# The FFN down product of a hybrid encoder layer: its sums in the order S3, S2, S1 and T3, T2, T1, and its products in that order

## The chip, the cores and the metric

One core of a Trainium2 chip runs the whole layer as one program. The metric is the device time of that core in microseconds (us), taken as the median of three runs.

## What is computed

The reference is one inference step of a streaming encoder layer on 1024 prompt rows and 32 sample rows: a combined input projection, latent attention beside an RWKV-7 state update, an output projection with a residual, and a SwiGLU feed-forward part. Everything is float32. The change touches the last step alone:

```python
def layer_tail(x, attn, rw, attn_out_g, w_out, norm_ffn_g, w_gate, w_up, w_down):
    mix = jnp.concatenate([rmsnorm(attn, attn_out_g), rw], axis=-1)
    h = x + mix @ w_out
    u = rmsnorm(h, norm_ffn_g)
    return h + (jax.nn.silu(u @ w_gate) * (u @ w_up)) @ w_down
```

The model width is 1024, the hidden width 2816, and there are 1056 rows.

## The kernel before

The function `tail` computes this last step, transposed: `hid` holds the hidden activations as 22 blocks of 128 partitions by 1056 rows, and `io.w_down` holds the weights by blocks of 128 output columns. The down product is done by the seven-product form of Strassen's method (Winograd's order of the sums), one level deep. The weights are split into A11, A12 (output blocks 0 to 3, hidden blocks 0 to 10 and 11 to 21) and A21, A22 (output blocks 4 to 7), the activations into B11, B12, B21, B22 by hidden half and row half. The sums are

- S1 = A21 + A22, S2 = S1 - A11, S3 = A11 - A21, S4 = A12 - S2, made by GpSimd (POOL), once in each round;
- T1 = B12 - B11, T2 = B22 - T1, T3 = B22 - B12, T4 = B21 - T2, made by VectorE (DVE), once for each of two column halves.

There are eight rounds n (list `DOWN`: two column halves `nh` by four output block pairs `j`). A round multiplies 128x128 blocks with 264 columns. It has seven products of 11 blocks (22 matmul instructions, since each block is given in two passes), which accumulate in four PSUM banks X, Y, Z and W; rounds alternate between two sets of four banks. Their names are those of the semaphores which they raise. In a round from the second on their order is

| product | operands | bank | what it waits for |
|---|---|---|---|
| q1 | A11, B11 | X | load `a11_in` |
| q6 | S2, T2 | Y | sums `e2_ok`, `f2_ok` |
| q7 | S3, T3 | Z | sums `e3_ok`, `f3_ok` |
| q5 | S1, T1 | W | stands behind q6, so nothing more |
| q4 | A22, T4 | Z | load `a22_in`, sum `f4_ok`, DVE's `q_u3` |
| q2 | A12, B21 | X | load `a12_in` |
| q3 | S4, B22 | W | sum `e4_ok`, DVE's `q_c22` |

In round 0, q2 stands right behind q1. DVE adds the products: u2 = Y + (a copy of q1's X), u3 = Z + u2, c22 = W + u3, then the four output tiles `yout`, each scaled and added to the residual tile `hres`.

What sets the order around the change is written out by hand, engine by engine:

- SyncE (SP) issues all loads from one queue in program order: A11 into `Alo[:, 0:FH]` (L2268), in round 0 also A12 (L2270), A21 into `Ahi[:, 0:FH]` (L2274), A22 into `Ahi[:, FH:]` (L2278), A12 into `Alo[:, FH:]` (L2282), then the stores of the round before (L2291) and the residual loads (L2294). There is one buffer of each; a load waits for the product and the sums that last read it. `FH` is 11.
- In round 0 A11 and A12 are loaded ahead of the end of the gate and up product, A21 and A22 behind its last product (`w_ps`).
- POOL makes the sums of a round in the order S1 (L2505, L2506: it lies in two places, so two instructions), S2 (L2510, L2511), S3 in place over A21 (L2512), S4 (L2517). Before S1 it waits for all of A11, A21 and A22.
- DVE makes T1 (L2642), T2 (L2643), T3 in place over B12 (L2644), T4 (L2647, L2648), for the first column half in front of round 0 and for the second within round 3.

All matmuls stand in the trace under line L2337 of a helper, and products are told apart by their tiles: q6 and q5 in one stretch are `psum<-mixT,u_sum`, q4 is `psum<-u_sum,wA`, q3 `psum<-hid,mixT`, and q1, q2 and q7 `psum<-hid,wA`. Where two products on the same tiles follow each other, one row shows the start of the first.

Of the kernel before, what the change touches and what calls it, by code (L numbers as in the profile page):

```python
# [7 lines left out]
ALU = mybir.AluOpType  # L8
# [2161 lines left out]
def tail(nc, g, io, phase):  # L2170
# [7 lines left out]
    FH, KH = FB // 2, KD // 2  # L2178
# [36 lines left out]
    S2d = u_sum[2][:, 0:FH * P].rearrange("p (k n) -> p k n", k=FH)  # L2215
# [15 lines left out]
    @block.sync  # L2231
    def _(sp):
        def load(u, b):
            sp.dma_start(wo[b], io.w_out[u]).then_inc(s[f"in{b}"], 16)

        for i, (a, b) in enumerate(X_PARTS):
            sp.dma_start(hT[:, a:b], io.x_cols[a:b].rearrange("k p n -> p k n")).then_inc(s[f"x_in{i}"], 16)
            if i:
                load(i + 1, i + 1)
        sp.dma_start(g_ffn[:, :], io.g_ffn).then_inc(s["g_in"], 16)  # L2240

        def load_unit(u):
            pair, b = u // 2, u % 2
            w = io.w_up if b else io.w_gate
            for a in range(2):
                sp.dma_start(ab[b][:, a], w[pair + a * FH]).then_inc(s[f"w_in{b}"], 16)

        load_unit(0)
        load_unit(1)
        for u in range(4, KD):  # L2250
            sp.wait_ge(s["ps_done"], 3 * (u - 3))
            load(u, u % 4)
        sp.wait_ge(s["h_ok"], 3 * KD)
        sp.dma_start(io.y.rearrange("k p n -> p k n"), hT).then_inc(s["h_st"], 16)
        for u in range(2, UNITS):
            sp.wait_ge(s["w_ps"], 2 * u - 2)
            load_unit(u)

        def rows(j):
            return io.w_down[j]  # L2260

        for n, (nh, j) in enumerate(DOWN):
            sp.wait_ge(s["w_ps"], 2 * UNITS - 2)
            if n:
                sp.wait_ge(s["q1_ps"], n)
                sp.wait_ge(s["e3_ok"], n)
                sp.wait_ge(s["e2_ok"], n)
            sp.dma_start(Alo[:, 0:FH], rows(j)[:, 0:FH]).then_inc(s["a11_in"], 16)  # L2268
            if n == 0:
                sp.dma_start(Alo[:, FH:], rows(j)[:, FH:]).then_inc(s["a12_in"], 16)  # L2270
            sp.wait_ge(s["w_ps"], 2 * UNITS)
            if n:
                sp.wait_ge(s["q7_ps"], n)
            sp.dma_start(Ahi[:, 0:FH], rows(j + KH)[:, 0:FH]).then_inc(s["a21_in"], 16)  # L2274
            if n:
                sp.wait_ge(s["q4_ps"], n)
                sp.wait_ge(s["e1_ok"], n)
            sp.dma_start(Ahi[:, FH:], rows(j + KH)[:, FH:]).then_inc(s["a22_in"], 16)  # L2278
            if n:
                sp.wait_ge(s["q2_ps"], n)  # L2280
                sp.wait_ge(s["e4_ok"], n)
                sp.dma_start(Alo[:, FH:], rows(j)[:, FH:]).then_inc(s["a12_in"], 16)  # L2282
            if n == 0:
                sp.wait_ge(s["h_st"], 16)
            else:
                sp.wait_ge(s["y_ok"], 3 * n)
                sp.wait_ge(s["q_x"], n)
                pn, pj = DOWN[n - 1]
                for a in range(4):
                    m, t0 = pj + KH * (a // 2), HT * (a % 2) + NW * pn  # L2290
                    sp.dma_start(io.y[m][:, t0:t0 + NW], yout[:, a, :]).then_inc(s["y_st"], 16)  # L2291
            for a in range(4):
                m, t0 = j + KH * (a // 2), HT * (a % 2) + NW * nh
                sp.dma_start(hres[:, a, :], io.y[m][:, t0:t0 + NW]).then_inc(s["res_in"], 16)  # L2294
        sp.wait_ge(s["y_ok"], 3 * len(DOWN))
        sp.wait_ge(s["q_x"], len(DOWN))
        pn, pj = DOWN[-1]
        for a in range(4):
            m, t0 = pj + KH * (a // 2), HT * (a % 2) + NW * pn
            sp.dma_start(io.y[m][:, t0:t0 + NW], yout[:, a, :]).then_inc(s["y_st"], 16)  # L2300
        sp.wait_ge(s["y_st"], 64 * len(DOWN))
        sp.wait_ge(s["h_st"], 16)

    @block.tensor
    def _(pe):
# [90 lines left out]
        for n, (nh, j) in enumerate(DOWN):  # L2396
            X, Y, Z, W = (4 * (n % 2) + i for i in range(4))
            c0, c1 = slice(nh * NW, nh * NW + NW), slice(HT + nh * NW, HT + nh * NW + NW)
            lo0, lo1 = (lambda k: hid[:, k, c0]), (lambda k: hid[:, k, c1])
            hi0, hi1 = (lambda k: hid[:, FH + k, c0]), (lambda k: hid[:, FH + k, c1])  # L2400
            left = lambda w: (lambda k: w[:, k, :])
            pe.wait_ge(s["a11_in"], 16 * n + 16)
            if n == 0:
                pe.wait_ge(s["hid_ok"], 6 * UNITS)
            if n >= 2:
                pe.wait_ge(s["q_x"], n - 1)
            product(X, left(Alo[:, 0:FH]), lo0, FH, "q1_ps")

            def x_close():
                pe.wait_ge(s["a12_in"], 16 * n + 16)  # L2410
                pe.wait_ge(s["q1_ok"], n + 1)
                product(X, left(Alo[:, FH:]), hi0, FH, "q2_ps", first=False)

            if n == 0:
                x_close()
            pe.wait_ge(s["e2_ok"], n + 1)
            pe.wait_ge(s["f2_ok"], nh + 1)
            if n >= 2:
                pe.wait_ge(s["q_u2"], n - 1)
            product(Y, left(S2d), lambda k: T2d[:, k, :], FH, "q6_ps")  # L2420
            pe.wait_ge(s["e3_ok"], n + 1)
            pe.wait_ge(s["f3_ok"], nh + 1)
            if n >= 2:
                pe.wait_ge(s["q_z"], n - 1)
            product(Z, left(Ahi[:, 0:FH]), lo1, FH, "q7_ps")
            if n >= 2:
                pe.wait_ge(s["q_w"], n - 1)
            product(W, lambda k: S1d[0][:, k, :] if k < 10 else S1d[1][:, k - 10, :], lambda k: T1d[:, k, :], FH, "q5_ps")
            pe.wait_ge(s["f4_ok"], nh + 1)
            pe.wait_ge(s["a22_in"], 16 * n + 16)  # L2430
            pe.wait_ge(s["q_u3"], n + 1)
            product(Z, left(Ahi[:, FH:]), lambda k: T4d[0][:, k, :] if k < 8 else T4d[1][:, k - 8, :], FH, "q4_ps", first=False)
            if n:
                x_close()
            pe.wait_ge(s["e4_ok"], n + 1)
            pe.wait_ge(s["q_c22"], n + 1)
            product(W, left(S4d), hi1, FH, "q3_ps", first=False)
# [44 lines left out]
    def _(pool):  # L2482
# [16 lines left out]
        for n in range(len(DOWN)):  # L2499
            pool.wait_ge(s["a11_in"], 16 * n + 16)  # L2500
            pool.wait_ge(s["a21_in"], 16 * n + 16)
            pool.wait_ge(s["a22_in"], 16 * n + 16)
            if n:
                pool.wait_ge(s["q5_ps"], n)
            tt(S1d[0], Ahi[:, 0:10], Ahi[:, FH:FH + 10], ALU.add)  # L2505
            tt(S1d[1], Ahi[:, 10:FH], Ahi[:, FH + 10:], ALU.add).then_inc(s["e1_ok"], 1)  # L2506
            pool.wait_ge(s["e1_ok"], n + 1)
            if n:
                pool.wait_ge(s["q6_ps"], n)
            tt(S2d[:, 0:10], S1d[0], Alo[:, 0:10], ALU.subtract)  # L2510
            tt(S2d[:, 10:], S1d[1], Alo[:, 10:FH], ALU.subtract).then_inc(s["e2_ok"], 1)  # L2511
            tt(Ahi[:, 0:FH], Alo[:, 0:FH], Ahi[:, 0:FH], ALU.subtract).then_inc(s["e3_ok"], 1)  # L2512
            pool.wait_ge(s["a12_in"], 16 * n + 16)
            pool.wait_ge(s["e2_ok"], n + 1)
            if n:
                pool.wait_ge(s["q3_ps"], n)
            tt(S4d, Alo[:, FH:], S2d, ALU.subtract).then_inc(s["e4_ok"], 1)  # L2517

    @block.vector
    def _(dve):  # L2520
        tt, stt = dve.tensor_tensor, dve.scalar_tensor_tensor

        def named(ins, name, value):
            ins.then_inc(s[name], 1)
            dve.wait_ge(s[name], value)
# [108 lines left out]
        for n, (nh, j) in enumerate(DOWN):  # L2634
            c0, c1 = slice(nh * NW, nh * NW + NW), slice(HT + nh * NW, HT + nh * NW + NW)

            def sums(nh):
                c0, c1 = slice(nh * NW, nh * NW + NW), slice(HT + nh * NW, HT + nh * NW + NW)
                B11, B12, B21, B22 = (hid[:, FH * a:FH * a + FH, c] for a in range(2) for c in (c0, c1))
                if nh:  # L2640
                    dve.wait_ge(s["q5_ps"], KH)
                named(tt(T1d, B12, B11, ALU.subtract), "f1_ok", nh + 1)  # L2642
                named(tt(T2d, B22, T1d, ALU.subtract), "f2_ok", nh + 1)  # L2643
                tt(B12, B22, B12, ALU.subtract).then_inc(s["f3_ok"], 1)  # L2644
                if nh:
                    dve.wait_ge(s["q4_ps"], KH)
                tt(T4d[0], B21[:, 0:8], T2d[:, 0:8], ALU.subtract)  # L2647
                tt(T4d[1], B21[:, 8:], T2d[:, 8:], ALU.subtract).then_inc(s["f4_ok"], 1)  # L2648
# [157 lines left out]
```

## Time and profile before

| | us |
|---|---|
| median of the runs (3) | 1897.72 |
| lowest and highest | 1897.05, 1898.7 |
| the profiled execution | 1898.8 |
| its span, first to last instruction | 1897.0 |
| TensorE matmul busy in the span | 1795.9 |
| VectorE busy | 955.3 |
| GpSimd busy | 691.5 |

The down product fills the last 290 us of the span or so. Start times are in us from the span's start. PE is the matmul, PEld the load of its weights, which runs just ahead of the matmul and marks where a product begins; PEclk is the granted clock of TensorE as a share of full speed.

### The profile page before, as it was taken

To read this page: it belongs to the slowest core of one execution; us is meant where nothing else is said; L and a number is where in the kernel's file an instruction comes from. 1 tells how busy PE (TensorE), PEld (TensorE's weight loads), DVE (VectorE), ACT (ScalarE), POOL (GpSimd) and SP (SyncE) were. 2 spreads that over 40 slices of the span, in tenths; PEclk is the share of its full clock that TensorE was granted. 3 is DMA by queue.
4 is the path that set the end of the run, shared out by engine and by line. 5 is a ranking of instruction groups with operands and counts; after the bars stand their busy time and mean duration, and the time that the engine had idled before them with its cause. 6 is when DMAs were issued, how large, how long until landed. Compare 5 with 4: busy or idle time off the path is not lost. (4 is left out here: it accounts for less than half of the span.)

```text
span 1897.0 us, 34197 instructions
## 1 busy us (share of the span) xinstructions
PE 1795.9 (95%) x14597; PEld 1336.5 (70%) x14597; DVE 955.3 (50%) x1710; ACT 384.9 (20%) x918; POOL 691.5 (36%) x495
## 2 busy tenths in 40 slices
PE   5999999999997987999899899999999999899998
PEld 3566666666665664555566788888888888688887
DVE  2757767766776773555333543343444334324422
ACT  2333333334333322333100111100001000000000
POOL 2553664555354534445320111222222220534522
PEclk9999999999997888999999999999999999999999
DMA  9343244324221006110130211101111112233331
GB/s 377 111 152 103 77 136 135 94 88 157 92 80 54 7 7 163 46 45 1 75 128 9 105 45 45 35 32 45 45 45 45 45 45 73 84 114 115 122 101 64
DMA packets 70906, 158.62 MB, mean 84 GB/s; under 512 B 19290, under 2 KB 47786, under 8 KB 66531
## 3 DMA queue, kind: packets, MB, share of 16 engines
q1 hardware_dynamic: 66866, 115.74, 19.0%
q10 hardware_dynamic: 3888, 40.70, 6.0%
q8 instruction: 116, 1.90, 0.4%
q14 instruction: 36, 0.29, 0.0%
HBM read 128.30 MB, written 20.44 MB: 78 GB/s over the span
## 5 line engine op out<-in xcount | busy, mean ns | idle before, releaser
L2337 PE MATMUL psum<-mixT,wA 128*128 128x264 f32 x1408 | 337.3, 388 | 1.9 <-DVE rb L2579 1.5
L2337 PEld LDWEIGHTS psum<-mixT,wA 128*128 128x128 f32 x1408 | 268.3, 191 | 48.6 <-DVE rb L2579 1.7
L2337 PE MATMUL psum<-u_sum,wA 128*128 128x264 f32 x1232 | 297.4, 386 | 0.5 <-DVE u_sum L2562 0.5
L437 PE MATMUL psum<-wsl,xt 128*128 128x368 f32 (+1 forms) x1092 | 283.8, 452 | 8.8 <-DMA wsl<-in_w_in 5.7
L2337 PEld LDWEIGHTS psum<-u_sum,wA 128*128 128x128 f32 x1232 | 234.3, 190 | 41.1 <-issue 0.9
L437 PEld LDWEIGHTS psum<-wsl,xt 128*128 128x128 f32 (+1 forms) x1092 | 150.0, 172 | 90.8 <-issue 18.1
L2492 POOL TENSOR_TENSOR wA<-wA 128x512 f32<-128x512 f32 x22 | 28.6, 1299 | 427.6 <-DMA wA<-in_w_gate 233.4
L2337 PE MATMUL psum<-hid,wA 128*128 128x264 f32 x528 | 121.6, 386 | 2.1 <-DVE hid L2630 1.5
L2337 PEld LDWEIGHTS psum<-hid,wA 128*128 128x128 f32 x528 | 100.2, 190 | 19.9 <-issue 2.8
L2505 POOL TENSOR_TENSOR u_sum<-wA 128x1280 f32<-128x1280 f32 x8 | 24.7, 3092 | 184.6 <-DMA wA<-in_w_down 184.6
L2337 PE MATMUL psum<-mixT,u_sum 128*128 128x264 f32 x352 | 82.9, 392 | 9.4 <-POOL u_sum L2511 9.4
L2130 DVE TENSOR_REDUCE part<-psum 128x1 f32<-128x80 f32 (+6 forms) x112 | 49.8, 470 | 76.2 <-PE psum L1924 73.8
L1278 POOL TENSOR_TENSOR Ls<-Lraw,con 128x512 f32<-128x512 f32 x45 | 49.2, 1102 | 106.5 <-ACT Lraw L945 76.5
L2337 PEld LDWEIGHTS psum<-mixT,u_sum 128*128 128x128 f32 x352 | 67.8, 193 | 22.4 <-POOL u_sum L2511 10.6
L1924 PE MATMUL psum<-kT,qT 96*128 96x144 f32 (+6 forms) x224 | 67.9, 463 | 7.8 <-DMA kT<-scratch_kT 7.8
L1244 POOL TENSOR_TENSOR st<-st,con 128x3 f32<-128x3 f32 (+1 forms) x18 | 50.7, 2816 | 60.2 <-DVE st L1441 30.7
L1943 PE MATMUL psum<-qT,kT 128*128 128x512 f32 (+6 forms) x224 | 71.4, 474 | 0.0
L2459 ACT ACTIVATE p<-psum 128x264 f32<-128x264 f32 x44 | 17.2, 390 | 253.6 <-PE psum L2337 253.4
L945 ACT ACTIVATE proj<-psum,rstd 128x368 f32<-128x368 f32 (+1 forms) x72 | 36.9, 512 | 136.5 <-PE psum L437 132.5
L1924 PEld LDWEIGHTS psum<-kT,qT 96*128 96x128 f32 x224 | 42.4, 197 | 30.0 <-DMA kT<-scratch_kT 7.9
L2092 POOL TENSOR_TENSOR tot<-tot,pT 128x832 f32<-128x832 f32 (+5 forms) x48 | 61.8, 1287 | 3.8
L1943 PEld LDWEIGHTS psum<-qT,kT 128*128 128x128 f32 x224 | 39.7, 183 | 31.5 <-issue 20.1
(362 smaller groups left out, 2875.9 us busy)
## 6 DMA issues: line engine op xcount, KB each, us to landing
wsl<-in_w_in ACTq DMA_DIRECT2D x27, 1472.0 KB, 6.9
wA<-in_w_down SPq DMA_DIRECT2D x32, 704.0 KB, 4.1
wA<-in_w_gate SPq DMA_DIRECT2D x22, 512.0 KB, 4.4
wA<-in_w_up SPq DMA_DIRECT2D x22, 512.0 KB, 4.4
mixed<-proj SPq DMA_DIRECT2D x8, 784.0 KB
xt<-in_x_tiles SPq DMA_DIRECT2D x9, 512.0 KB, 6.0
wsl<-in_w_in SPq DMA_DIRECT2D x3, 1472.0 KB, 11.3
out_y<-hid SPq DMA_DIRECT2D x1, 4224.0 KB, 12.0
```

The costliest lines, as they stand in the source:

```text
L437: return pe.matmul(out, lhsT, rhs, start=start, stop=stop)
L945: copy = lambda out, in_, **k: act.activation(out, in_, ACT.Copy, **k)
L1244: tt(out, ms, c_("minus_half")[:, 0:n], ALU.pow).then_inc(s[ok], 1)
L1278: tt(Ls[i % 2][:, :, :], Lraw[:, :, :], bcast(c_("levels")[:, i * 64:(i + 1) * 64], 1, H), ALU.mult).then_inc(s["Ls_ok"], 1)
L1924: pe.matmul(bank(pos)[:, 0:y - x], qT[b][0:QKD, t * P:(t + 1) * P], kT[b][0:QKD, x:y], start=True, stop=True).then_inc(s["a_ps"], 1)
L1943: pe.matmul(bank(pos)[0:size[k], 0:y - x], kT[b][:, k * P:k * P + size[k]], qT[b][:, x:y], start=True, stop=True).then_inc(s["b_ps"], 1)
L2092: step(pool.tensor_tensor(out[:, first[k]:], out[:, first[k]:], p[:, at[k]:at[k + 1]], ALU.add))
L2130: last = dve.tensor_reduce(part[:, t, slot:slot + 1], src[:, 0:w], AX.X, ALU.max)
L2337: ins = pe.matmul(pb[bank][:, 0:NW], left(k), right(k), start=first and k == 0, stop=k == depth - 1, skip_group_check=not first)
L2459: act.activation(p1_[it % 2][:, :], pb[X][:, 0:NW], ACT.Copy).then_inc(s["p1_ok"], 1)
L2492: tt(S1, A21, A22, ALU.add).then_inc(s["s1_ok"], 1)
L2505: tt(S1d[0], Ahi[:, 0:10], Ahi[:, FH:FH + 10], ALU.add)
```

## The change

POOL makes S3 first, S2 from it (S2 = A22 - S3) and S1 last (S1 = S2 + A11); S2 is one instruction in place of two. DVE makes T3 first, T2 from it (T2 = T3 + B11) and T1 last (T1 = B22 - T2). TensorE runs q7, q6, q5 in place of q6, q7, q5, and q5 has waits of its own for S1 and T1. POOL waits for A22 only behind S3. SP's waits follow: the load of A11 waits for S1, the loads of A21 and A22 for S2. The seven products, their operands and their number are the same.

```diff
@@ block.sync
             if n:
                 sp.wait_ge(s["q1_ps"], n)
                 sp.wait_ge(s["e3_ok"], n)
-                sp.wait_ge(s["e2_ok"], n)
+                sp.wait_ge(s["e1_ok"], n)
             sp.dma_start(Alo[:, 0:FH], rows(j)[:, 0:FH]).then_inc(s["a11_in"], 16)
...
             if n:
                 sp.wait_ge(s["q7_ps"], n)
+                sp.wait_ge(s["e2_ok"], n)
             sp.dma_start(Ahi[:, 0:FH], rows(j + KH)[:, 0:FH]).then_inc(s["a21_in"], 16)
             if n:
                 sp.wait_ge(s["q4_ps"], n)
-                sp.wait_ge(s["e1_ok"], n)
+                sp.wait_ge(s["e2_ok"], n)
             sp.dma_start(Ahi[:, FH:], rows(j + KH)[:, FH:]).then_inc(s["a22_in"], 16)
@@ block.tensor
+            pe.wait_ge(s["e3_ok"], n + 1)
+            pe.wait_ge(s["f3_ok"], nh + 1)
+            if n >= 2:
+                pe.wait_ge(s["q_z"], n - 1)
+            product(Z, left(Ahi[:, 0:FH]), lo1, FH, "q7_ps")
             pe.wait_ge(s["e2_ok"], n + 1)
             pe.wait_ge(s["f2_ok"], nh + 1)
             if n >= 2:
                 pe.wait_ge(s["q_u2"], n - 1)
             product(Y, left(S2d), lambda k: T2d[:, k, :], FH, "q6_ps")
-            pe.wait_ge(s["e3_ok"], n + 1)
-            pe.wait_ge(s["f3_ok"], nh + 1)
-            if n >= 2:
-                pe.wait_ge(s["q_z"], n - 1)
-            product(Z, left(Ahi[:, 0:FH]), lo1, FH, "q7_ps")
+            pe.wait_ge(s["e1_ok"], n + 1)
+            pe.wait_ge(s["f1_ok"], nh + 1)
             if n >= 2:
                 pe.wait_ge(s["q_w"], n - 1)
@@ block.gpsimd
             pool.wait_ge(s["a21_in"], 16 * n + 16)
+            tt(Ahi[:, 0:FH], Alo[:, 0:FH], Ahi[:, 0:FH], ALU.subtract).then_inc(s["e3_ok"], 1)
             pool.wait_ge(s["a22_in"], 16 * n + 16)
+            pool.wait_ge(s["e3_ok"], n + 1)
+            if n:
+                pool.wait_ge(s["q6_ps"], n)
+            tt(S2d, Ahi[:, FH:], Ahi[:, 0:FH], ALU.subtract).then_inc(s["e2_ok"], 1)
+            pool.wait_ge(s["e2_ok"], n + 1)
             if n:
                 pool.wait_ge(s["q5_ps"], n)
-            tt(S1d[0], Ahi[:, 0:10], Ahi[:, FH:FH + 10], ALU.add)
-            tt(S1d[1], Ahi[:, 10:FH], Ahi[:, FH + 10:], ALU.add).then_inc(s["e1_ok"], 1)
-            pool.wait_ge(s["e1_ok"], n + 1)
-            if n:
-                pool.wait_ge(s["q6_ps"], n)
-            tt(S2d[:, 0:10], S1d[0], Alo[:, 0:10], ALU.subtract)
-            tt(S2d[:, 10:], S1d[1], Alo[:, 10:FH], ALU.subtract).then_inc(s["e2_ok"], 1)
-            tt(Ahi[:, 0:FH], Alo[:, 0:FH], Ahi[:, 0:FH], ALU.subtract).then_inc(s["e3_ok"], 1)
+            tt(S1d[0], S2d[:, 0:10], Alo[:, 0:10], ALU.add)
+            tt(S1d[1], S2d[:, 10:], Alo[:, 10:FH], ALU.add).then_inc(s["e1_ok"], 1)
             pool.wait_ge(s["a12_in"], 16 * n + 16)
-            pool.wait_ge(s["e2_ok"], n + 1)
@@ block.vector
-                named(tt(T1d, B12, B11, ALU.subtract), "f1_ok", nh + 1)
-                named(tt(T2d, B22, T1d, ALU.subtract), "f2_ok", nh + 1)
-                tt(B12, B22, B12, ALU.subtract).then_inc(s["f3_ok"], 1)
+                named(tt(B12, B22, B12, ALU.subtract), "f3_ok", nh + 1)
+                named(tt(T2d, B12, B11, ALU.add), "f2_ok", nh + 1)
+                tt(T1d, B22, T2d, ALU.subtract).then_inc(s["f1_ok"], 1)
```

## Rows read from the trace of the kernel before

**Rows 1.** The page's chain that ended last: shares of the span by engine.

```profile
PE 7%; DVE 0%; POOL 0%; issue 0%
```

**Rows 2.** Waits of TensorE from 1600 us on: total us, times, longest us.

```profile
PE psum L2337 <- POOL u_sum L2511: 9.4, 3, 7.7
```

**Rows 3.** Timeline, round 0: start us, duration us, engine, line, tiles, count, idle before.

```profile
1604.82 3.18 DVE L2642 TENSOR_TENSOR mixT<-hid 128x2904 f32<-128x2904 f32 x1
...
1608.04 3.18 DVE L2643 TENSOR_TENSOR mixT<-hid,mixT 128x2904 f32<-128x2904 f32 x1
...
1610.34 3.63 POOL L2505 TENSOR_TENSOR u_sum<-wA 128x1280 f32<-128x1280 f32 x1 [46.51 <-DMA wA<-in_w_down]
1610.61 4.75 PEld L2337 LDWEIGHTS psum<-hid,wA 128*128 128x128 f32 x22 [0.96 <-issue]
...
1611.25 5.76 DVE L2644 TENSOR_TENSOR hid<-hid 128x2904 f32<-128x2904 f32 x1
1613.93 3.39 POOL L2506 TENSOR_TENSOR u_sum<-wA 128x128 f32<-128x128 f32 x1
1616.93 2.60 DVE L2647 TENSOR_TENSOR u_sum<-hid,mixT 128x2112 f32<-128x2112 f32 x1
1617.40 4.87 POOL L2510 TENSOR_TENSOR u_sum<-u_sum,wA 128x1280 f32<-128x1280 f32 x1
1619.46 3.65 DVE L2648 TENSOR_TENSOR u_sum<-hid,mixT 128x792 f32<-128x792 f32 x1
1622.24 1.19 POOL L2511 TENSOR_TENSOR u_sum<-u_sum,wA 128x128 f32<-128x128 f32 x1
...
1623.48 6.41 PEld L2337 LDWEIGHTS psum<-mixT,u_sum 128*128 128x128 f32 x22 [8.13 <-POOL u_sum L2511]
...
1629.93 4.86 PEld L2337 LDWEIGHTS psum<-hid,wA 128*128 128x128 f32 x22
...
1639.72 4.86 PEld L2337 LDWEIGHTS psum<-u_sum,wA 128*128 128x128 f32 x22
```

**Rows 4.** DMA issues of 1603.4 to 1603.7 and 1603.8 to 1604.2: us to landing.

```profile
wA<-in_w_down SPq DMA_DIRECT2D x1, 704.0 KB, 4.7
...
wA<-in_w_down SPq DMA_DIRECT2D x1, 704.0 KB, 6.1
```

**Rows 5.** Busy time by stretch: length, PE, PEld, DVE, ACT, POOL, PEclk, DMA, GB/s.

```profile
1616.00:1623.50 7.50, 0.02 (x1) 0.02 (x1) 7.12 (x3) 0.00 (x0) 7.42 (x4) 0.77 0.00 0
1623.50:1627.00 3.50, 3.50 (x8) 2.78 (x9) 0.00 (x0) 0.00 (x0) 3.50 (x2) 0.52 0.02 5
...
1650.00:1660.00 10.00, 8.48 (x39) 6.93 (x38) 3.02 (x3) 0.39 (x1) 9.92 (x6) 1.00 0.36 114
```

**Rows 6.** Timeline of round 1, with the load of A22 ahead of it.

```profile
1645.03 0.33 SPq L2278 DMA_DIRECT2D wA<-in_w_down  x1
...
1649.30 2.90 POOL L2505 TENSOR_TENSOR u_sum<-wA 128x1280 f32<-128x1280 f32 x1 [19.62 <-DMA wA<-in_w_down]
1649.51 4.86 PEld L2337 LDWEIGHTS psum<-hid,wA 128*128 128x128 f32 x22
...
1655.80 0.45 POOL L2511 TENSOR_TENSOR u_sum<-u_sum,wA 128x128 f32<-128x128 f32 x1
...
1656.30 4.75 PEld L2337 LDWEIGHTS psum<-mixT,u_sum 128*128 128x128 f32 x22 [1.93 <-POOL u_sum L2511]
...
1661.08 4.86 PEld L2337 LDWEIGHTS psum<-hid,wA 128*128 128x128 f32 x22
```

**Rows 7.** Timeline of round 4: starts of q1 and q7.

```profile
1754.09 4.86 PEld L2337 LDWEIGHTS psum<-hid,wA 128*128 128x128 f32 x22
...
1764.30 4.86 PEld L2337 LDWEIGHTS psum<-hid,wA 128*128 128x128 f32 x22
```

**Rows 8.** POOL's sums by line over all rounds: ns min/median/max, first and last start.

```profile
L2506 POOL TENSOR_TENSOR u_sum<-wA x8: 645/647/3390, 1613.9 to 1855.2; 128x128 f32<-128x128 f32 x8
...
L2512 POOL TENSOR_TENSOR wA<-wA x8: 3152/3349/3352, 1623.4 to 1859.4; 128x1408 f32<-128x1408 f32 x8
```

**Rows 9.** Timeline of round 2: issue of the next round's load of A11.

```profile
1691.80 0.33 SPq L2268 DMA_DIRECT2D wA<-in_w_down  x1
```

## The prediction, made before the changed kernel was run

> **What bounds the kernel now.** I read the chain that ended last, then TensorE's waits in the down product, then the timeline around each wait, then the granted clock there. The chain is TensorE's [rows 1], so only time in which TensorE stands still, or runs at the lower clock, is worth anything. From 1600 us on it waits for one POOL line in any amount: 9.4 us in 3 pieces, the longest 7.7 us, all for the second instruction of S2 [rows 2]. The reader should see where the pieces lie, from the starts of products. An undisturbed product takes 4.89 us (q7 starts at 1629.93 and q4, two products on, at 1639.72: 9.79 for two), or 4.78 when it starts from rest (1656.30 to 1661.08) [rows 3, 6].
>
> - Round 0: q2 starts at 1610.61, q7 at 1629.93 [rows 3]. Between lie q2 and q6, worth 9.79; the round loses 19.32 - 9.79 = 9.53 us. This is the wait for S2, whose last piece ends at 1622.24 + 1.19 = 1623.43, and a slow q6: from 1623.48 to 1629.93 it takes 6.45 instead of 4.78, so 1.67 us of the loss is clock. PEclk is 0.52 from 1623.5 to 1627 (the 1.2 GHz level), after TensorE had stood still nearly the whole 7.5 us before [rows 5].
> - Round 1: q1 starts at 1649.51, q7 at 1661.08 [rows 6]: 11.57 - 9.79 = 1.78 us. The clock stayed at 1.00 through this gap [rows 5].
> - Round 4: 1754.09 to 1764.30 [rows 7]: 0.42 us.
>
> The sum is 11.73 us, and this is all that an order of sums can win here; the other five rounds show no wait.
>
> **The change part by part.** *Why S2 is late in round 0.* S1 cannot start before A22 has landed (1610.34), and then four POOL instructions stand ahead of q6. They are also slow: the 128-element piece of S1 took 3.39 us where its median is 0.65 [rows 3, 8]. The timeline shows why. DVE's T3 was issued at 1611.25 but ended 1617.01, 3.04 us after POOL's instruction ended (1613.97); POOL's 128 elements then ended 0.31 us after T3. POOL and DVE take turns, one whole instruction each, whenever both operands of DVE lie in SBUF. So I lay out the new order as one queue, with the durations that an instruction has from the moment it gets its turn [rows 3]: DVE's 2904 columns 3.04, its 2112 columns 2.21 (1617.32 to 1619.53), its 792 columns 0.84 (1622.27 to 1623.11), POOL's 1280 columns 2.75, its 128 columns 0.31. POOL's 1408 columns take 3.15 alone [rows 8]; less the 0.15 by which 1280 columns shorten (2.90 [rows 6] to 2.75) that is 3.0.
>
> *Round 0 after.* T3 takes T1's place, 1604.82 to 1608.00, and T2 starts at 1608.04 and ends 1611.22, as now. A21 was issued at the start of the 1603.4 to 1603.7 stretch and lands 4.7 us later [rows 4], so at about 1608.2: S3 finds T2 running. Taking turns from there: S3 ends 1614.2, T1 1617.3, S2 1620.3, first part of T4 1622.5, first part of S1 1625.2, second part of T4 1626.1, last of S1 1626.4. TensorE: q2 starts at 1610.61 as now, q7 at 1615.39 (S3 and T3 are there), q6 is due at 1620.28 and gets S2 at 1620.3, q5 is due at 1625.2 and waits for S1 until 1626.4, q4 starts 4.78 later at 1631.2 (T4 is there). Now q4 starts at 1639.72 [rows 3]. **Saving 8.5 us**; of the loss of 9.53 some 1.0 stays, moved from q6 to q5. S4, right behind S1, ends about 1629.4 to 1629.8 and is wanted at 1636. Bounds of this term: if POOL got its turn for S3 before T2, S1 would end a turn of DVE earlier, at 1625.4, and nothing is left to wait for: 9.5. If every turn cost its full standalone duration instead of the shortened one (0.14 or 0.15 more for each of the five longer turns behind T2, 0.34 and 0.39 for the two short ones, 1.5 in all), S1 would end at 1627.9: 7.0. I take 8.5, the value of turns as measured.
>
> *Rounds 1 to 7.* A22 is still the last load, issued when q4 ends (1645.03) and usable 4.27 us later (1649.30) [rows 6]. Now S1 and S2 must be done when q2, q3 and q1 are, 14.7 us after q4; in round 1, where q2 had gone ahead, two products only, hence its wait. After the change S2 is the first sum behind A22 and wanted one product later, behind q7: even with the worst POOL instruction of the trace, 4.87 [rows 3], it is there after 4.3 + 4.9 = 9.2 us, wanted after 14.7 us (round 1) or 19.6 (others). S1 is wanted a product later still; all four present pieces of S1 and S2 at their worst sum to 13.1 [rows 3], so it is there by 17.4, wanted at 19.6 or 24.5. Round 1 saves **1.8 us**, round 4 **0.4 us**.
>
> *What moves on SP's queue.* The next load of A11 now waits for S1, the last of three sums, where it waited for S3, also the last of three. Now it is issued at 1691.80 in round 2 [rows 9], whose q1 began at 1649.51 + 1.78 + 7 x 4.89 = 1685.5, so 6.3 us into the round. By the bound above S1 ends at the latest 17.4 us after q4, 7.6 us into the round. The load then lands by about 14 (6.1 us at worst, rows 4) and is wanted at 34. The load of A21 stands behind it and behind q7, now a product earlier (9.8 us into the round); S3 then falls into q5, ends by about 22 with two turns of POOL and DVE, and is wanted at 39. Behind them in SP's queue nothing is nearer its time than now. The new waits on S2 are met long before the products they stand beside. On DVE u2 now waits for the later of the two products, and u3 follows at once: 0.9 us of DVE inside q5's 4.89.
>
> **Sum.** 8.5 + 1.8 + 0.4 = 10.7 us. The profiled execution takes 1898.8 us and would take 1888.1; the median of the runs lies 1.1 us below it, so I predict **1887.0 us**.
>
> **The rivals.**
>
> - *Nothing is left of the wait* (20%). S3 gets its turn before T2, because A21 is there before 1608.0 or because the turns fall otherwise. For it: it takes only 0.2 us. Against: the landing time. It saves 11.7: **1886.0**.
> - *The short wait for S1 lowers the clock* (8%). 1.67 us as in round 0 now, so **1888.7**. Against: the 1.5 us gap of round 1 left it at 1.00 [rows 5]. Beside this stands the Trainium skill, TensorE: Matmul & The Clock Gate, "What's actually happening": the half-rate state is the default, and recent activity lifts it. By that rule a gap in front of q5 could be charged again and the saving would be 9.0; the trace agrees that a long gap is charged, and for a short one shows none.
> - *DVE keeps its turn for the chain of T sums* (5%). T2, T1 and T4 run on to about 1618.0, S3 ends at 1621.0, q7 waits 5.6 us, S2 and S1 are then in time. The saving is 9.53 - 5.6 + 2.2 = 6.1: **1891.6**. Against: POOL did get its turn between T2 and T3 [rows 3]. The Trainium skill, SBUF — State Buffer, "Who interferes with whom", speaks against the change in the same direction: of a DVE instruction with two SBUF inputs and a GpSimd one that reads SBUF, the later to issue blocks fully. By its words alone the three sums of POOL stay bound to DVE's three; the trace agrees (5.76 against 3.18), and without the blocking the sum would be 11.7.
> - *The change does less than it says* (4%). TensorE's gap in round 0 keeps a cause that I don't see, and only rounds 1 and 4 gain: 2.2 us, **1895.5**.
> - *Slower: the loads start late in every round* (3%). Place: SP's queue. The store of `yout` and the residual loads stand ahead of the load of A11, and behind POOL's later sums DVE's last tiles could be late, so A11 would miss q1 of the next round. It decides once A11 is issued later than about 28 us into a round, where I find 7.6 at worst; then each us is paid in seven rounds. At 30 us: 7 x 2 = 14 us lost, 10.7 won: **1901**.
>
> My forecast has 60%.
>
> **How the numbers follow.** The range takes in the forecast with both bounds of its main term (7.0 to 9.5, so 1886.0 to 1888.5), the first two rivals, the 0.8 us or so by which the runs spread (1897.05 to 1898.7), and a little of the third: 1885.2 to 1889.9. It leaves out some 12 to 15%. A measurement of this kernel can tell about 0.2% from no change, 3.8 us: faster means below 1893.9. Faster has the forecast and three rivals, 93%; the same 4%; slower 3%.
>
> **What would show it.** Right: no wait of TensorE for POOL's second sum; q7 of round 0 some 4.8 us behind q2's start; a wait of about 1 us in front of q5 of round 0 and for S1; PEclk at 1.00 throughout the down product; no gaps in rounds 1 to 7; the T and S instructions of round 0 in turns. Wrong: q7 of round 0 waits for S3, or any gap in rounds 1 to 7, above all at q1 for A11.

## The result and the profile after

The changed kernel takes 1885.53 us (median of 6 runs, 1882.91 to 1886.79) against 1898.03 us of the kernel before measured with it; the ratio is 0.9931, interval 0.9918 to 0.9943. That is 12.5 us, where 10.7 were forecast. On the scale of the 1897.72 us that the prediction started from, the ratio gives 1884.6 us, just under the range's lower end of 1885.2. The interval in us is 10.8 to 15.6, so the forecast 10.7 lies just outside it. Two later measurements of the same kernel gave 0.9946 (0.9932 to 0.9960) and 0.9950 (0.9936 to 0.9963), and both of these intervals hold 10.7. The question of this study is where the first one's extra 1.8 us came from.

First, what the change did. The timeline of round 0 after it, the answer to [rows 3] (start us, duration us, engine, line, tiles, count, idle before):

```profile
1599.59 3.18 DVE L2644 TENSOR_TENSOR hid<-hid 128x2904 f32<-128x2904 f32 x1
...
1602.81 3.18 DVE L2645 TENSOR_TENSOR mixT<-hid 128x2904 f32<-128x2904 f32 x1
1603.49 5.52 POOL L2505 TENSOR_TENSOR wA<-wA 128x1408 f32<-128x1408 f32 x1 [44.64 <-DMA wA<-in_w_down]
...
1605.37 9.64 PEld L2338 LDWEIGHTS psum<-hid,wA 128*128 128x128 f32 x44 [0.96 <-issue]
...
1606.03 6.03 DVE L2646 TENSOR_TENSOR mixT<-hid,mixT 128x2904 f32<-128x2904 f32 x1
1609.16 5.92 POOL L2510 TENSOR_TENSOR u_sum<-wA 128x1408 f32<-128x1408 f32 x1
1611.98 5.32 DVE L2649 TENSOR_TENSOR u_sum<-hid,mixT 128x2112 f32<-128x2112 f32 x1
1615.13 4.78 PEld L2338 LDWEIGHTS psum<-mixT,u_sum 128*128 128x128 f32 x22
1615.16 4.88 POOL L2514 TENSOR_TENSOR u_sum<-u_sum,wA 128x1280 f32<-128x1280 f32 x1
...
1617.21 3.67 DVE L2650 TENSOR_TENSOR u_sum<-hid,mixT 128x792 f32<-128x792 f32 x1
1620.01 1.19 POOL L2515 TENSOR_TENSOR u_sum<-u_sum,wA 128x128 f32<-128x128 f32 x1
...
1621.25 4.75 PEld L2338 LDWEIGHTS psum<-mixT,u_sum 128*128 128x128 f32 x22 [1.34 <-POOL u_sum L2515]
...
1626.03 4.86 PEld L2338 LDWEIGHTS psum<-u_sum,wA 128*128 128x128 f32 x22
```

Read it from the start of DVE's first T sum (T3, L2644, at 1599.59; before it was T1, at 1604.82): everything stands 5.23 us earlier. q2 and q7 are one row of 44 weight loads, since S3 (L2505, done 1609.01) and T3 are there in time. q6 (1615.13) starts 0.05 us behind the end of S2 (L2510, done 1615.08): as laid out, the two come due together, and S2 has no time to spare. q5 waits for the last piece of S1 (L2515, done 1621.20) and starts at 1621.25. Add 5.23 to compare with the layout in the prediction:

| ends, on the scale of before | laid out | measured |
|---|---|---|
| S3 | 1614.2 | 1614.24 |
| T1 | 1617.3 | 1617.29 |
| S2 | 1620.3 | 1620.31 |
| T4, first part | 1622.5 | 1622.53 |
| S1, first part | 1625.2 | 1625.27 |
| S1, last part | 1626.4 | 1626.43 |
| q4 starts | 1631.2 | 1631.26 |

TensorE's waits in the down product, the answer to [rows 2] (total us, times, longest us):

```profile
PE psum L2338 <- DVE hid L2632: 1.5, 1, 1.5
PE psum L2338 <- POOL u_sum L2515: 0.9, 1, 0.9
PE psum L2338 <- ACT p L2482: 0.6, 1, 0.6
```

The first and third were there before and are not touched. The second is the wait for S1 that the prediction expected; no other piece is left of the 9.4 us. The clock, the answer to [rows 5] (length, then busy time of PE, PEld, DVE, ACT, POOL, then PEclk, DMA, GB/s):

```profile
1599.00:1616.00 17.00, 15.73 (x70) 13.15 (x71) 16.90 (x6) 0.39 (x1) 12.29 (x3) 1.00 0.34 119
1616.00:1622.00 6.00, 5.08 (x23) 4.04 (x22) 5.66 (x4) 0.00 (x0) 6.00 (x3) 1.00 0.00 0
1622.00:1640.00 18.00, 18.00 (x82) 15.38 (x81) 9.91 (x11) 0.00 (x0) 10.19 (x4) 1.00 0.44 161
1640.00:1660.00 20.00, 20.00 (x91) 17.07 (x91) 4.12 (x6) 0.39 (x1) 8.63 (x4) 1.00 0.37 126
1660.00:1881.00 221.00, 216.06 (x972) 184.15 (x970) 72.12 (x91) 2.34 (x6) 79.86 (x29) 1.00 0.32 104
```

PEclk is 1.00 throughout, on both sides of the wait of 0.9 us. From 1622 to 1660 TensorE is busy all of the time; this takes in the step from round 0 to round 1 and the place of round 1's old gap (round 1 itself runs to 1670.08). In the later rounds the sums come long before they are wanted, as in these rows of rounds 1 and 2 (load of A22, S2, q1 of round 2, load of A11):

```profile
1660.71 0.33 SPq L2279 DMA_DIRECT2D wA<-in_w_down  x1
...
1664.90 3.16 POOL L2510 TENSOR_TENSOR u_sum<-wA 128x1408 f32<-128x1408 f32 x1 [9.45 <-DMA wA<-in_w_down]
...
1670.08 9.76 PEld L2338 LDWEIGHTS psum<-hid,wA 128*128 128x128 f32 x44
...
1675.95 0.33 SPq L2268 DMA_DIRECT2D wA<-in_w_down  x1
```

S2 of round 2 is done 7.35 us after the end of q4 (9.2 was the bound) and wanted by q6 at 1679.87. The next load of A11 goes out 5.9 us into round 2 (7.6 was the bound).

From the start of q1's first matmul to the end of the span the profiled execution before takes 1897.0 - 1604.93 = 292.1 us, the one after 1881.1 - 1599.70 = 281.4 us. The difference is the forecast **10.7 us**. But the two spans differ by 15.9: the other 5.2 us lie ahead of the down product, where no instruction was changed.

### The profile page after: what moved, and what is told of

The parts are those of the page before. It is cut to its first block, busy times and chain, and to the rows that moved or that the text cites. A ratio compares the mean times of both kernels' runs of the same rounds, so it can differ in the third digit from the quotient of the medians.

```text
span 1881.1 us, 34196 instructions
## 1 busy us (share of the span) xinstructions
PE 1792.1 (95%) x14597; PEld 1334.9 (71%) x14597; DVE 963.1 (51%) x1710; ACT 384.6 (20%) x918; POOL 691.1 (37%) x487
## 4 chain that ended last, share of the span: by engine, by line
PE 48%; POOL 1%; DVE 1%; DMA 0%; issue 0%; POOLq 0%; DVEq 0%
PE psum L2338 42%; PE psum L2317 5%; POOL u_sum L2510 0%; POOL wA L2505 0%; DMA wA<-in_w_down 0%; POOL u_sum L2514 0%; PE psum L2327 0%; DVE u_sum L2564 0%; DVE u_sum L2569 0%; DVE mixT L2565 0%; PE psum L2333 0%; DVE mixT L2548 0%; DVE rb L2581 0%; DVE hid L2545 0%; DVE hid L2544 0%; POOL u_sum L2515 0%
## 5 line engine op out<-in xcount | busy, mean ns | idle before, releaser
L1924 PE MATMUL psum<-kT,qT 96*128 96x144 f32 (+6 forms) x224 | 67.5, 461 | 7.7 <-DMA kT<-scratch_kT 7.7
L2505 POOL TENSOR_TENSOR wA<-wA 128x1408 f32<-128x1408 f32 x8 | 27.8, 3477 | 109.0 <-DMA wA<-in_w_down 109.0
L1924 PEld LDWEIGHTS psum<-kT,qT 96*128 96x128 f32 x224 | 42.2, 196 | 29.9 <-DMA kT<-scratch_kT 7.8
```

The lines of the kernel that those rows point to most:

```text
L1924: pe.matmul(bank(pos)[:, 0:y - x], qT[b][0:QKD, t * P:(t + 1) * P], kT[b][0:QKD, x:y], start=True, stop=True).then_inc(s["a_ps"], 1)
```

## The experiments

Two questions were put. Theory A says that the 5.2 us ahead of the down product differ from execution to execution, whatever the kernel; theory B, that the changed program shortens that part. And the gain in the down product itself was taken apart, to see whether its three gaps and the turns of POOL and DVE are what they were taken for. The length of the down product (first matmul of q1 to the end of the span) is taken from each profile; it is free of what happens ahead of it.

### The unchanged kernel again

No edit.

> The unchanged kernel once more, beside itself. Theory A (the change saves 10.7 us in the down product alone; the 5.2 us by which the profiled execution of the changed kernel reached the down product earlier, 1599.7 against 1604.9, come from how the clock of TensorE happens to fall between 570 and 640 us): ratio 1.000, single times over some 3 us, and the profile's down product starts anywhere from 1599 to 1606 us with the same length as before, 292.1 us from q1's start to the span's end. Theory B (the changed program itself shortens the part ahead of the down product): the start is again at 1604.9 within 0.5, and the times stay within 1 us.

Measured: ratio 1.000 (0.9991 to 1.001); 11 runs from 1893.7 to 1901.37 us, 7.7 us apart. The down product takes 291.9 us (292.1 before) and its T1 (L2642) starts at 1601.2, where the first profile has 1604.82:

```profile
L2642 DVE TENSOR_TENSOR mixT<-hid x2: 3182/3182/3183, 1601.2 to 1736.6; 128x2904 f32<-128x2904 f32 x2
```

The part ahead of the down product moved by 3.6 us with nothing changed. Theory B's fixed start is gone. Theory A's spread was itself too small: 3 us were expected and 7.7 seen.

### The changed kernel again, twice

No edit.

> The changed kernel once more. Theory A: 10.7 us less than the kernel before in the median, 1887.3 against 1898.0 (ratio 0.9944) within about 1 us, a down product of 281.4 us in the profile, and a start of it that differs from 1599.7 by more than 0.5 us. Theory B: 12.5 to 15.9 us less again (ratio 0.9916 to 0.9934), with the start at 1599.7.

> The changed kernel a third time. By theory A (10.7 us in the down product, the rest is where the clock of TensorE falls between 570 and 640 us): 10.7 us less than the kernel before, ratio 0.9944 within 0.0012, a down product of 281.4 us, and again another start of it. By theory B (something beside the down product is shorter): a ratio of 0.9934 or less.

Measured: 1887.11 us against 1897.43 (ratio 0.9946), then 1888.30 against 1898.16 (0.9950). The down product takes 281.4 us both times, as in the first profile, and its T3 starts at 1601.3 and at 1607.0, where it had been 1599.6. The median of all 18 runs is 1886.81 us. By theory B the ratio should have been 0.9934 or less; the interval of the second of these measurements excludes that, the interval of the first just reaches it. Two rows of each profile, before, after, and the second and third time of after, show where the part ahead differs; L508 is run first and last near 55 and 576 us, L1924 begins the attention. In each row the two times are the first and the last start:

```profile
L508 PE MATMUL psum<-con,area x9: 272/273/478, 54.9 to 576.6; 128*128 128x128 f32 x9
L1924 PE MATMUL psum<-kT,qT x224: 284/454/874, 724.5 to 881.7; 96*128 96x264 f32 x16, 96*128 96x328 f32 x16, 96*128 96x392 f32 x16, 96*128 96x456 f32 x16
```

```profile
L508 PE MATMUL psum<-con,area x9: 272/273/473, 54.2 to 576.0; 128*128 128x128 f32 x9
L1924 PE MATMUL psum<-kT,qT x224: 285/454/874, 719.9 to 876.6; 96*128 96x264 f32 x16, 96*128 96x328 f32 x16, 96*128 96x392 f32 x16, 96*128 96x456 f32 x16
```

```profile
L508 PE MATMUL psum<-con,area x9: 272/273/404, 53.6 to 575.3; 128*128 128x128 f32 x9
L1924 PE MATMUL psum<-kT,qT x224: 284/454/874, 721.0 to 878.1; 96*128 96x264 f32 x16, 96*128 96x328 f32 x16, 96*128 96x392 f32 x16, 96*128 96x456 f32 x16
```

```profile
L508 PE MATMUL psum<-con,area x9: 272/273/473, 57.1 to 578.7; 128*128 128x128 f32 x9
L1924 PE MATMUL psum<-kT,qT x224: 284/454/874, 726.6 to 883.8; 96*128 96x264 f32 x16, 96*128 96x328 f32 x16, 96*128 96x392 f32 x16, 96*128 96x456 f32 x16
```

| stretch, us | before | after | after, 2nd | after, 3rd |
|---|---|---|---|---|
| start to L508 | 54.9 | 54.2 | 53.6 | 57.1 |
| L508 first to last | 521.7 | 521.8 | 521.7 | 521.6 |
| L508 last to L1924 | 147.9 | 143.9 | 145.7 | 147.9 |
| L1924 to the down product's first T sum | 880.3 | 879.7 | 880.3 | 880.4 |

The long stretches agree within 0.7 us. What varies is the first 55 us, by 3.5 us, and the 145 us behind the last L508, by 4.0 us, and the third profile of the changed kernel is as long in the latter as the kernel before. So the extra 5.2 us of the first pair of profiles are 4.0 from that one stretch, 0.7 from the beginning and the rest in small amounts: theory A. In the stretch the clock of TensorE is not steady (before, then after: PEclk is the third number from the end):

```profile
570.00:640.00 70.00, 53.41 (x937) 42.05 (x939) 45.76 (x76) 21.33 (x42) 30.34 (x21) 0.72 0.13 37
```

```profile
570.00:640.00 70.00, 55.47 (x1003) 43.84 (x996) 48.94 (x80) 22.70 (x44) 32.38 (x22) 0.75 0.12 32
```

The changed kernel's first execution had more of the full clock there (0.75 against 0.72) and got through 1003 matmuls in the window against 937. Over all ten profiles of this study the four shortest of these stretches (143.1 to 145.7 us) have a PEclk of 0.74 to 0.77 from 570 to 640 us, the six longer ones (146.3 to 147.9 us) 0.70 to 0.72; within each group the order is not strict. So length and clock go together, but that the clock is the cause of the 4 us is argued, not shown. What makes the first 55 us differ was not followed up.

### Round 0 alone, and the other rounds alone

The choice between old and new order is made per round, for the products, for POOL's sums (on `n`) and for DVE's (on `nh`), and the loads of A11, A21 and A22 wait for all three sums (the line numbers of the trace move with each edit). For round 0 alone, with the bodies of both orders as in the two kernels:

```diff
+            if n == 0:
...
+                product(Z, left(Ahi[:, 0:FH]), lo1, FH, "q7_ps")
...
+                product(Y, left(S2d), lambda k: T2d[:, k, :], FH, "q6_ps")
+            else:
...
+                product(Y, left(S2d), lambda k: T2d[:, k, :], FH, "q6_ps")
...
+                product(Z, left(Ahi[:, 0:FH]), lo1, FH, "q7_ps")
...
+                if nh == 0:
+                    named(tt(B12, B22, B12, ALU.subtract), "f3_ok", nh + 1)
...
+                else:
+                    named(tt(T1d, B12, B11, ALU.subtract), "f1_ok", nh + 1)
```

> The new order in round 0 and for the T sums of the first half alone; the other rounds and the second half as before. Theory of three separate gaps: 8.5 us of the 10.7 are won, the down product takes 283.6 us, and the gaps of rounds 1 (1.8 us) and 4 (0.4 us) are back or, in round 1, partly gone where the earlier loads help. Rival (round 0's gain comes back as waits in the later rounds if these keep their order): more than 285 us.

Measured: the down product takes 283.6 us, 8.5 less than 292.1; 1889.54 us against 1897.43, ratio 0.9956 (0.9945 to 0.9968). The gap of round 1 is back in full:

```profile
1640.34 4.86 PEld L2341 LDWEIGHTS psum<-hid,wA 128*128 128x128 f32 x22
1647.15 4.75 PEld L2341 LDWEIGHTS psum<-mixT,u_sum 128*128 128x128 f32 x22 [1.95 <-POOL u_sum L2542]
1651.93 4.86 PEld L2341 LDWEIGHTS psum<-hid,wA 128*128 128x128 f32 x22
```

From q1 (1640.34) to q7 (1651.93) are 11.59 us, as in [rows 6], instead of 9.79. So is that of round 4, with 10.20 us from q1 to q7:

```profile
1744.93 4.86 PEld L2341 LDWEIGHTS psum<-hid,wA 128*128 128x128 f32 x22
...
1755.13 4.86 PEld L2341 LDWEIGHTS psum<-hid,wA 128*128 128x128 f32 x22
```

The other half has the same edit with the conditions turned round (`if n`, `if nh`).

> The other half of the change: the old order in round 0 and for the first half's T sums, the new order in rounds 1 to 7 and for the second half. Theory of three separate gaps: round 0 loses its 9.5 us as before, rounds 1 and 4 lose nothing, the down product takes 292.1 - 1.8 - 0.4 = 289.9 us. Rival (the later gaps are a consequence of round 0's): 291 or more.

Measured: 289.9 us, 2.2 less than 292.1; 1894.97 us against 1898.16, ratio 0.9985 (0.9973 to 0.9997). TensorE's waits show the wait of round 0 and none behind it:

```profile
PE psum L2341 <- POOL u_sum L2542: 7.7, 1, 7.7
PE psum L2341 <- DVE hid L2661: 1.5, 1, 1.5
PE psum L2341 <- ACT p L2497: 0.6, 1, 0.6
```

The two halves add up: 8.5 + 2.2 = 10.7. The gaps are separate, and their sizes are those of the prediction.

### The S sums in the new order, the T sums in the old

Here too the loads of A11, A21 and A22 wait for all three S sums. Beside that the edit is, in effect:

```diff
-                named(tt(B12, B22, B12, ALU.subtract), "f3_ok", nh + 1)
-                named(tt(T2d, B12, B11, ALU.add), "f2_ok", nh + 1)
-                tt(T1d, B22, T2d, ALU.subtract).then_inc(s["f1_ok"], 1)
+                named(tt(T1d, B12, B11, ALU.subtract), "f1_ok", nh + 1)
+                named(tt(T2d, B22, T1d, ALU.subtract), "f2_ok", nh + 1)
+                tt(B12, B22, B12, ALU.subtract).then_inc(s["f3_ok"], 1)
```

> The new order of the S sums and of the products, but DVE's T sums in the old order T1, T2, T3. By the turns: T3 is the third DVE sum, ends behind S3's turn, and q7 of round 0 waits for it about 1.9 us; S1 ends as late as in the changed kernel and q5 finds it there. So one wait takes the place of the other, and the down product takes 282.0 us against 281.4. Rival (the order of the T sums doesn't matter since DVE is far ahead): 281.4, with the wait in front of q5. Rival (DVE's order is half of the gain): over 285.

Measured: 282.1 us; 1889.02 us against 1898.16, ratio 0.9953 (0.9939 to 0.9967).

```profile
1609.05 5.68 POOL L2508 TENSOR_TENSOR wA<-wA 128x1408 f32<-128x1408 f32 x1 [44.79 <-DMA wA<-in_w_down]
...
1611.74 6.03 DVE L2654 TENSOR_TENSOR hid<-hid 128x2904 f32<-128x2904 f32 x1
...
1617.89 4.75 PEld L2341 LDWEIGHTS psum<-hid,wA 128*128 128x128 f32 x22 [2.05 <-issue]
1617.92 5.13 PE L2341 MATMUL psum<-hid,wA 128*128 128x264 f32 x22 [1.66 <-DVE hid L2654]
...
1622.67 9.76 PEld L2341 LDWEIGHTS psum<-mixT,u_sum 128*128 128x128 f32 x44
```

q7 waits for T3 (L2654, which ends at 1617.77 because S3, L2508, had the turn ahead of it until 1614.73), and q6 and q5 then follow without a wait. Nearly all of the gain is the order of the S sums and of the products; the order of the T sums, with the S sums in the new order, is worth 0.7 us.

### T4 behind S1, and S4 behind T4

In the changed kernel q5 waits because T4, which is wanted only by q4, takes turns ahead of S1. The first edit holds T4 of the first half back.

```diff
                 if nh:
                     dve.wait_ge(s["q4_ps"], KH)
+                else:
+                    dve.wait_ge(s["e1_ok"], 1)
```

> The changed kernel, with DVE's T4 of the first column half held back until S1 of round 0 is done. Theory of turns at one port (each SBUF instruction of POOL and DVE waits for the other's): S1 loses the turns of T4 ahead of it and is done about 2.5 to 3 us earlier, behind S2 by 2.75 + 0.65; q5 of round 0 doesn't wait (now 1.3 us); the down product takes 280.4, 1.0 us less than the changed kernel's 281.4. Rival (POOL is slow by itself there, or the wait is something else): S1 ends as late as now, and the down product stays at 281.4.

Measured: 280.9 us, not 280.4. The expected part came true: S1's first part takes 2.89 us in place of 4.88, its second 0.46 in place of 1.19, and q5 follows q6 without a wait. But a new wait stands in front of q4:

```profile
1619.24 9.68 PEld L2338 LDWEIGHTS psum<-mixT,u_sum 128*128 128x128 f32 x44
1619.27 2.89 POOL L2514 TENSOR_TENSOR u_sum<-u_sum,wA 128x1280 f32<-128x1280 f32 x1
...
1622.11 0.46 POOL L2515 TENSOR_TENSOR u_sum<-u_sum,wA 128x128 f32<-128x128 f32 x1
1622.53 3.20 POOL L2519 TENSOR_TENSOR mixT<-wA,u_sum 128x1408 f32<-128x1408 f32 x1
1622.60 5.34 DVE L2651 TENSOR_TENSOR u_sum<-hid,mixT 128x2112 f32<-128x2112 f32 x1 [6.44 <-POOL u_sum L2515]
...
1629.76 4.75 PEld L2338 LDWEIGHTS psum<-u_sum,wA 128*128 128x128 f32 x22 [0.84 <-issue]
1629.79 5.13 PE L2338 MATMUL psum<-u_sum,wA 128*128 128x264 f32 x22 [0.45 <-DVE part L2663]
```

POOL's S4 (L2519) stands right behind S1 and took the turn ahead of T4 (L2651, 5.34 us, S4's 3.20 among them). DVE's u2 and u3 stand behind T4, and q4 waits for u3 (L2663). 1887.75 us against 1897.43 (ratio 0.9944, 0.9931 to 0.9957): the times alone can't tell this kernel from the changed one, the lengths in the profiles do (280.9, 281.4). The second edit adds to the first that S4 of round 0, which is wanted only by q3, goes behind T4:

```diff
             if n:
                 pool.wait_ge(s["q3_ps"], n)
+            else:
+                pool.wait_ge(s["f4_ok"], 1)
             tt(S4d, Alo[:, FH:], S2d, ALU.subtract).then_inc(s["e4_ok"], 1)
```

> As the run with T4 held back until S1 is done, and POOL's S4 of round 0 held back until T4 is done. Theory of turns at one port: there the wait in front of q5 was gone, but S4 took the turn ahead of T4 (its first part took 5.3 us in place of 2.4), DVE's u2 and u3 stood behind T4, and q4 lost 0.6 us to u3. With S4 behind T4, T4 is done about 3.4 us behind S1, u3 some 1.3 us after that, ahead of q4, and S4 some 7 us ahead of q3: no wait in round 0, a down product of 280.3 us against 281.4 of the changed kernel. Rival (u2 and u3 are late for another reason than the turn that S4 took): q4 still waits about 0.6 us and the down product stays at 280.9.

Measured: 280.2 us; 1884.59 us against 1898.16, ratio 0.9929 (0.9917 to 0.9941). T4's first part takes 2.36 us, S4 goes last, and q4 follows q5 without a wait:

```profile
1616.69 9.68 PEld L2338 LDWEIGHTS psum<-mixT,u_sum 128*128 128x128 f32 x44
...
1620.05 2.36 DVE L2653 TENSOR_TENSOR u_sum<-hid,mixT 128x2112 f32<-128x2112 f32 x1 [6.44 <-POOL u_sum L2515]
...
1623.45 3.19 POOL L2521 TENSOR_TENSOR mixT<-wA,u_sum 128x1408 f32<-128x1408 f32 x1 [3.43 <-DVE u_sum L2654]
...
1626.40 4.86 PEld L2338 LDWEIGHTS psum<-u_sum,wA 128*128 128x128 f32 x22
```

This kernel leaves no wait for a sum in the down product, and its down product is the shortest: 1.2 us under the changed kernel's and 11.9 under the one before, about all of the 11.73 that the prediction gave as the most that an order of sums can win. In the same measurement the changed kernel had 1888.30 us, 3.7 us more. The profiles account for 1.2 of them; that the other 2.5 are again the part ahead is likely, not shown.

## Why the prediction was right and where it was wrong

**The mechanism, right.** That the three gaps are separate was shown by the two halves: 8.5 and 2.2 us, forecast as 8.5 and 1.8 + 0.4. That POOL's turns set the end of S1 was shown by the two edits that moved them. The layout of round 0 by turns came out to 0.07 us. The wait moved from q6 to q5, forecast at about 1.0 us: from the start of q6 (1615.13) to that of q4 (1626.03) are 10.90 us in place of 9.79, so 1.1. The clock stayed at 1.00, no gap is left in rounds 1 to 7, and SP's queue is within its bounds.

**The rivals.** That nothing would be left of the wait, that the short wait lowers the clock, that DVE keeps its turn, that the loads come late: the profile after excludes each (one wait of 0.9 us, PEclk 1.00, turns in strict order, A11 issued 5.9 us into the round). That round 0 would keep its gap is excluded by the 8.5 us of round 0 alone. The Trainium skill, SBUF — State Buffer, "Who interferes with whom", says that a DVE instruction with two SBUF inputs contends with a GpSimd instruction that reads SBUF, and that the order of issue decides which of the two is blocked. The trace agrees (T1 took 6.03 us and S2 5.92, each about a turn of the other engine's and one of its own, 3.0 each), and with both engines waiting in turn it was the alternation, seen in the rows of before, that set the order.

**What was wrong: the allowance for the spread of the runs.** The step that failed is the one in which the range took "the 0.8 us or so by which the runs spread" from three runs. With more runs the unchanged kernel lay between 1892.53 and 1900.67 us (17 runs), 8.1 us apart, and the part ahead of the down product alone moved by 3.6 us between two profiles of it. The median of the first six runs of the changed kernel was 1.3 us below that of its 18 (1885.53, 1886.81), and so the first ratio said 13 and the first medians 12.5 us. All runs on record, 51 of the unchanged kernel and 18 of the changed one, have means of 1897.35 and 1886.74 us, 10.6 apart, beside the forecast 10.7. The interval of the first ratio is 2.4 us wide to either side: that, and not 0.8, was the allowance to make for six runs against six. So the first six runs were a low draw. That it was chance is the simplest reading and not shown: the chip of the experiments is on record (11 and 7), that of the first measurement is not, and a difference between chips is not excluded. The chances by sign were not touched by this.

**Smaller faults.** The prediction set its sum against the profiled execution's 1898.8 us, but did not ask whether that execution's own part ahead of the change was a usual one. One profile shows a stage's length to 0.1 us or so where the stage is fixed by its own waits (281.4 us in three of three), and the whole only as one draw. The chain of [rows 1] covers only the last 7% of the span, which is from round 4 on, so it does not show that TensorE is the limit in rounds 0 and 1; the two halves do. And the 0.39 us by which the lower bound of 7.0 makes T4's second part dearer is 1.23 - 0.84, where the row of 1.23 us (L2648 in round 4) itself waited for a turn; in the last kernel above, with no POOL instruction in its way, that part took 0.98 us, so the bound is about 0.25 us too low.

## What to carry to other kernels

Where two engines take turns, as POOL and DVE do here, lay their instructions out as a single queue with the durations that an instruction has once it gets its turn: here that gave the end of each sum to less than 0.1 us, and it shows what else stands in the queue ahead of the sum that is wanted. Put the sum first that needs the fewest loads, and hold back those that are wanted late on both engines, since holding back one lets the other engine's take its turn. Compare the length of the stage that was changed, from a profile of each kernel, and take the spread of the total from many runs, not from three.

## What the runs showed of the hardware that was not expected

- The part of the program that was not changed is not the same from run to run: the first 55 us differ by 3.5 us, and the stretch from 576 to 725 us by 4.8 over the ten profiles (143.1 to 147.9), where PEclk from 570 to 640 us lies between 0.70 and 0.77. In the four profiles compared above the rest ahead of the down product repeats within 0.7 us in 1400; the down product repeats within 0.2 us in 292.
- A lead of 0.07 us decided who got a turn: in the kernel with T4 held back, the end of S1 let both S4 (next in POOL's order) and T4 go, S4 was issued at 1622.53 and T4 at 1622.60, and T4's first part then took 5.34 us in place of 2.36. Holding back T4 alone won 0.5 us of the down product (280.9 against 281.4), holding back S4 as well 1.2 (280.2).
